# A quarter of each low part moved from VectorE to GpSimd in a float32 decoder trunk

## The chip, the cores and the metric

The kernel runs on one core of one Trainium2 chip. The metric is the device time of one execution in microseconds (us), the median over runs; lower is better.

## The reference

The reference is a decoder trunk in float32: 256 tokens of width 1024 pass through four layers. Cut to what matters:

```python
for i in range(4):
    x = x + 0.5 * swiglu(rms_norm(x, g[i, 0]), w_gate[i, 0], w_up[i, 0], w_down[i, 0])
    h = rms_norm(x, g[i, 1])
    q, k, v = split(h @ w_qkv[i], 3)
    mix = attention_i(q, k, v)           # stick-breaking, differential, forgetting, stick-breaking
    x = x + mix @ w_o[i]
    x = x + 0.5 * swiglu(rms_norm(x, g[i, 2]), w_gate[i, 1], w_up[i, 1], w_down[i, 1])
return rms_norm(x, final_g)
```

`swiglu(x)` is `(silu(x @ w_gate) * (x @ w_up)) @ w_down` with a hidden width of 2816. The weights are float32 and each is used once per execution.

## The kernel before

**Chunks.** All weights lie in DRAM as one stream of 328 chunks, each 128 partitions x 2048 float32 columns (1 MB). A feed-forward phase uses 33 chunks (for each of 11 units of the hidden width a `top` and a `bottom` chunk with gate and up columns, and a `down` chunk), an attention phase 16 (`v`, `q`, `k`, `o`). There are 12 phases: feed-forward, attention, feed-forward in each of the four layers. The chunk that opens a phase is called c0 here, the ones behind it c0+1, c0+2 and so on; the chunks are used in the order of the stream (`FFN_ORDER`, `ATT_ORDER`).

**Split in high and low parts.** A float32 product is made of three products in the rounded format `fp32r`: high x high, high x low, low x high. Each chunk c goes through four stations:

- SyncE issues its DMA into `raw[c % 3]` (`load`, L281), once the low part of chunk c-3 has been taken, since that frees the buffer. The first 12 loads are written out, the rest run in a hardware loop (L299 to L302).
- ScalarE rounds it into `w_hi[c % 6]` (`hi`, L338), after `slot_free` has seen TensorE finish with chunk c-6. It counts `hi_ready`.
- VectorE takes `w_lo = raw - w_hi` over all 2048 columns (`lo`, L548), after `hi_ready`. It counts `lo_ready`.
- TensorE waits for `lo_ready` and multiplies. `product` (L902 to L904) issues the three matmuls.

Chunk 0 is done in two halves (`first_hi`, `first_lo`, L344 to L347 and L555 to L559).

**What sets the order.** Every engine runs one list of instructions that is written out by hand; `split_to(c)` and `split_next(k)` put the `hi` and `lo` of coming chunks at fixed places between an engine's other work. VectorE's other work is: the elementwise product of the hidden activations (`scratch`, L612), the low part of the activations (`m_lo`, L591 in feed-forward, L702 and L720 in attention), the residual update (`x`, L828), the gained and turned input (`wide`, L834) and its low part (`xg`, L840), and in attention the scaling of q and k (`q_t`, `k_t`, L682), the rotation (L690 to L692), masks and row sums.

**GpSimd** has one task: the power -0.5 of the mean square, two elements for each partition (`r_col`, L318 for the 12 phases, L321 for the two at the end). It waits for `mean_ready`, which VectorE counts in `norm_mean` (L570). In a phase, VectorE's order is: low part of c0+2, `norm_mean`, low parts of c0+3 and c0+4 (in attention `norm_diag`, L576, which waits for `r_col`, stands between `norm_mean` and c0+3). The low parts of c0 and c0+1 are taken near the end of the phase before.

**Waits.** An instruction carries one wait itself; a further wait on the same engine is an instruction of its own (EVENT_SEMAPHORE in the trace).

Of the kernel before, what the change touches and what calls it, by code (L numbers as in the profile page):

```python
# [8 lines left out]
F32 = mybir.dt.float32  # L9
F32R = mybir.dt.float32r  # L10
ALU = mybir.AluOpType
# [13 lines left out]
FFN_CHUNKS = 3 * UNITS  # L25
ATT_CHUNKS = 4 * PAIRS
# [4 lines left out]
HALF_D = D // 2  # L31
FIRST_KS = DT // 2
PEELED = 4
RAW = 3
RING = 6
SCALE = HD ** -0.5
# [63 lines left out]
def trunk(nc, stream, x_in, gains, consts, lam_in, subln_in, wf_in, bf_in, final_in, out):  # L100
    with ExitStack() as ctx:
# [3 lines left out]
        def sem(name):  # L105
            return ctx.enter_context(nc.semaphore(name))
# [43 lines left out]
        ones_loaded, const_loaded, gain_loaded = sem("ones_loaded"), sem("const_loaded"), sem("gain_loaded")  # L150
        x_loaded = sem("x_loaded0"), sem("x_loaded1")
        hi_ready = sem("hi_ready")
        lo_ready = sem("lo_ready")
        top_used = sem("top_used")
        acc_ready = sem("acc_ready")
        x_updated = sem("x_updated")
# [121 lines left out]
        @block.sync  # L278
        def _(sp):
            def load(c, chunk):  # L280
                sp.dma_start(raw[:, c % RAW, :], stream[chunk]).then_inc(raw_loaded[c % RAW], 16)  # L281

            sp.dma_start(cst[:, 0:C_LATER], consts[:, 0:C_LATER]).then_inc(ones_loaded, 16)
            sp.dma_start(gain[:], gains).then_inc(gain_loaded, 16)
            for half in range(2):
                cols = slice(half * HALF_D, (half + 1) * HALF_D)
                sp.dma_start(x[:, :, cols], x_in[:, :, cols]).then_inc(x_loaded[half], 16)
                part = slice(half * HALF, (half + 1) * HALF)
                sp.dma_start(raw[:, 0, part], stream[0, :, part]).then_inc(raw_loaded[0] if half else raw_half_loaded, 16)
            for c in range(1, RAW):  # L290
                load(c, c)
            for c in range(RAW, PEELED * RAW):
                sp.wait_ge(lo_ready, c - RAW + 1)
                load(c, c)
            for tile, source in ((cst[:, C_LATER:], consts[:, C_LATER:]), (lam_q[:], lam_in), (subln[:], subln_in),
                                 (wf[:], wf_in), (bf[:], bf_in), (final_gain[:], final_in)):
                sp.dma_start(tile, source).then_inc(const_loaded, 16)
            rounds = CHUNKS // RAW - PEELED
            with sp.Fori(0, rounds) as turn:  # L299
                for k in range(RAW):  # L300
                    sp.wait_ge(lo_ready, turn * RAW + ((PEELED - 1) * RAW + k + 1))
                    load(RAW + k, turn * RAW + (PEELED * RAW + k))  # L302
            for c in range((rounds + PEELED) * RAW, CHUNKS):
                sp.wait_ge(lo_ready, c - RAW + 1)
                load(c, c)
            for i, bank in enumerate(banks_of(NORMS - 1)):
                cols = slice(bank // TB * HALF_D, (bank // TB + 1) * HALF_D)
                sp.wait_ge(y_ready, i + 1)
                sp.dma_start(out[:, bank % TB, cols], x_part(bank)).then_inc(stored, 16)
            sp.wait_ge(stored, 16 * BANKS)  # L310

        @block.gpsimd
        def _(pool):
            nc.gpsimd.memset(half_neg[:], -0.5).then_inc(const_ready, 1)
            pool.wait_ge(const_ready, 1)
            for n in range(NORMS - 1):
                pool.wait_ge(mean_ready, n + 1)
                nc.gpsimd.tensor_tensor(r_col[:], mean[:], half_neg[:], ALU.pow).then_inc(r_col_ready, 1)  # L318
            for tb in range(TB):
                pool.wait_ge(mean_ready, NORMS + tb)  # L320
                nc.gpsimd.tensor_tensor(r_col[:, tb:tb + 1], mean[:, tb:tb + 1], half_neg[:, tb:tb + 1],  # L321
                                        ALU.pow).then_inc(r_col_ready, 1)
# [212 lines left out]
        def _(dve):  # L535
# [9 lines left out]
            def lo(c, turn=0):  # L545

                dve.wait_ge(hi_ready, c + 1 + turn * RING)
                nc.vector.tensor_tensor(w_lo[:, c % RING, :], raw[:, c % RAW, :], w_hi[:, c % RING, :].bitcast(F32),  # L548
                                        ALU.subtract).then_inc(lo_ready, 1)

            def first_lo(half):
# [347 lines left out]
        def _(pe):  # L899
# [52 lines left out]
            def ffn(layer, n, c0, _, f):  # L952
# [25 lines left out]
                def first_step(u):  # L978

                    turn_part(n, 2)  # L980
                    pe.wait_ge(lo_ready, c0 + 1)
                    pe.wait_ge(xg_ready, BANKS * n + 1)
                    gate_up(u, 0, c0, top)
                    turn_part(n, 3)
                    pe.wait_ge(xg_ready, BANKS * n + 2)
                    gate_up(u, 1, c0, top).then_inc(top_used, 1)

                def step(s, c, turn):
                    u = f * UNITS + s
                    if s == 0:  # L990
                        first_step(u) if n else very_first_step(u)
                    else:
                        pe.wait_ge(lo_ready, c + 1 + turn * RING)
                        gate_up(u, 0, c, top)
                        gate_up(u, 1, c, top).then_inc(top_used, 1)
                        hidden(u - 1, turn)
                    pe.wait_ge(lo_ready, c + 2 + turn * RING)
                    for tb in range(TB):
                        if s == 0:
                            pe.wait_ge(xg_ready, BANKS * n + 3 + tb)  # L1000
                        gate_up(u, tb, c + 1, bottom).then_inc(gu_psum, 1)
                    if s == UNITS - 1:
                        unit_down(s - 1, c + 2, turn, (0, 1))
                        hidden(u, turn)
                        unit_down(s - 1, c + 2, turn, (2, 3)).then_inc(down_used, 1)
                    elif s:
                        unit_down(s - 1, c + 2, turn).then_inc(down_used, 1)
# [9 lines left out]
                def unit_down(s, c, turn, banks=(0, 1, 2, 3)):  # L1017
                    u = f * UNITS + s
                    if banks[0] == 0:
                        pe.wait_ge(lo_ready, c + 1 + turn * RING)  # L1020
                        pe.wait_ge(h_split, u + 1 + turn * 2)
                    return contract_pair(c, u % 2 * 2, s == 0, banks)

                def last_down():
                    u, c = f * UNITS + UNITS - 1, c0 + FFN_CHUNKS - 1
                    pe.wait_ge(lo_ready, c + 1)
                    pe.wait_ge(h_split, u + 1)
                    contract_last(c, u % 2 * 2, n + 1)

# [5 lines left out]
            def attention(layer, n, c0, _, kind):  # L1035
# [5 lines left out]
                def values(js):  # L1041

                    half = js[0] // 2
                    for part in range(2):
                        c = c0 + ATT_ORDER.index(("v", 2 * half + part))
                        pe.wait_ge(lo_ready, c + 1)
                        for j in js:
                            tokens = slice(j % TB * P, (j % TB + 1) * P)
                            if half == 0:
                                pe.wait_ge(xg_ready, BANKS * n + TB * part + j + 1)  # L1050
                            for k in range(part * FIRST_KS, (part + 1) * FIRST_KS):
                                ins = product(work[:, V_BANK[j], :], xg_hi[:, k, tokens], xg_lo[:, k, tokens],
                                              wide_chunk(w_hi, c)[:, k % FIRST_KS, :],
                                              wide_chunk(w_lo, c)[:, k % FIRST_KS, :], start=k == 0, stop=k == DT - 1)
                            if part:
                                ins.then_inc(v_psum, 1)
                            elif j == 0:
                                turn_part(n, 3)
# [15 lines left out]
                def head_projection(c, bank, h):  # L1074

                    pe.wait_ge(lo_ready, c + 1)
                    ins = project(work[:, bank, h * T:(h + 1) * T], c, h * P)
                    if h:
                        ins.then_inc(qk_psum, 1)
# [74 lines left out]
                def output(j, banks=(0, 1, 2, 3)):  # L1154
                    c, b = c0 + ATT_ORDER.index(("o", j)), first + j
                    if banks[0] == 0:
                        pe.wait_ge(lo_ready, c + 1)
                        pe.wait_ge(mix_ready, b + 1)
                    if j == PAIRS - 1:
                        contract_last(c, 2 * (b % 2), n + 1)  # L1160
                        return
                    ins = contract_pair(c, 2 * (b % 2), j == 0, banks)
                    if banks[-1] == 3:
                        ins.then_inc(out_used, 1)
# [125 lines left out]
```

## Time and profile before

| | us |
|---|---|
| median of 3 runs | 1994.91 (1994.75 to 1997.24) |
| the profiled execution's own time | 1994.82 |
| its span in the profile | 1993.0 |
| TensorE busy (matmuls) | 1963.7, 99% of the span |
| VectorE busy | 1089.1, 55% |
| ScalarE busy | 918.9, 46% |
| GpSimd busy | 25.5, 1% |
| mean granted TensorE clock | 0.994 of full speed |

The span is what the profiler saw from the first to the last instruction; the execution's own time is 1.8 us longer. Times in rows count from the start of the span. PE is TensorE (matmuls), PEld its weight loads, DVE is VectorE, ACT ScalarE, POOL GpSimd, SP SyncE.

### The profile page before, as it was taken

Reading aid. Unit: us, or ns where it says so; the run is one execution under the profiler, and the core shown is the slowest. Engines: PE = TensorE matmul, PEld = TensorE weight load, DVE = VectorE, ACT = ScalarE, POOL = GpSimd, SP = SyncE. Lnnn points to the kernel's source line nnn. Section 1 sums busy time; section 2 is a strip of 40 time slices with the busy share of each in tenths; the row PEclk is TensorE's granted clock in tenths of the full one; section 3 lists DMA queues with packets and bytes.
Section 4 is the critical chain, followed back from the end, with each engine's and each line's share of the span. In section 5 each row is a group of like instructions: output and inputs, shape, how many; then the busy total and the mean of one; then the engine's idle time right before and its main releaser. Section 6 shows DMA issues by size and latency. Waiting matters only on the chain.

```text
span 1993.0 us, 24383 instructions
## 1 busy us (share of the span) xinstructions
PE 1963.7 (99%) x9684; PEld 1651.2 (83%) x9684; DVE 1089.1 (55%) x999; ACT 918.9 (46%) x942; POOL 25.5 (1%) x19
## 2 busy tenths in 40 slices
PE   7999999999999999999999999999999999999998
PEld 5888898888888888788888889988888888988886
DVE  5544566554644567644465554764446455646444
ACT  5444565444544445544444443454444444555442
POOL 0000000000000000000000000000000000000000
PEclk9999999999999999999999998999999999999999
DMA  6554444454455452454545542545554544535551
GB/s 248 212 186 189 165 151 170 183 185 185 184 190 189 148 190 106 151 188 188 189 182 185 184 166 106 181 162 186 188 190 183 183 185 165 190 127 190 188 186 69
DMA packets 49711, 348.58 MB, mean 175 GB/s; under 512 B 6128, under 2 KB 6256, under 8 KB 7792
## 3 DMA queue, kind: packets, MB, share of 16 engines
q1 hardware_dynamic: 49648, 347.67, 47.3%
q8 instruction: 48, 0.79, 0.2%
q14 instruction: 15, 0.12, 0.0%
HBM read 346.60 MB, written 1.05 MB: 174 GB/s over the span
## 4 chain that ended last, share of the span: by engine, by line
PE 96%; DVE 2%; ACT 1%; issue 0%; DMA 0%; SPq 0%; DVEq 0%; POOLq 0%; POOL 0%; ACTq 0%
PE work L902 20%; PE work L904 20%; PE work L903 20%; PE acc L902 9%; PE acc L904 9%; PE acc L903 9%; PE work L1013 2%; PE acc L945 1%; DVE w_lo L548 1%; PE work L1142 1%; PE work L1129 0%; PE work L1069 0%; PE work L1120 0%; PE work L1084 0%; PE work L1143 0%
## 5 line engine op out<-in xcount | busy, mean ns | idle before, releaser
L548 DVE TENSOR_TENSOR w_lo<-raw,w_hi 128x2048 fp32r<-128x2048 f32 x327 | 741.6, 2289 | 224.2 <-ACT w_hi L338 224.2
L338 ACT ACTIVATE w_hi<-raw 128x2048 fp32r<-128x2048 f32 x327 | 613.8, 1906 | 19.7 <-DMA raw<-stream_dram 19.5
L902 PE MATMUL work<-w_hi,xg 128*128 128x512 f32 x1536 | 609.4, 397 | 7.5 <-DVE w_lo L559 3.8
L904 PE MATMUL work<-w_hi,xg 128*128 128x512 f32 x1536 | 600.5, 391 | 0.0
L903 PE MATMUL work<-w_lo,xg 128*128 128x512 f32 x1536 | 599.7, 390 | 0.0
L902 PEld LDWEIGHTS work<-w_hi,xg 128*128 128x128 f32 x1536 | 289.4, 188 | 65.9 <-DVE w_lo L555 4.1
L904 PEld LDWEIGHTS work<-w_hi,xg 128*128 128x128 f32 x1536 | 289.2, 188 | 62.0
L903 PEld LDWEIGHTS work<-w_lo,xg 128*128 128x128 f32 x1536 | 289.5, 188 | 57.4
L902 PE MATMUL acc<-w_hi,m_hi 128*128 128x512 f32 x832 | 330.0, 397 | 4.4 <-DVE m_lo L720 4.4
L904 PE MATMUL acc<-w_hi,m_lo 128*128 128x512 f32 x832 | 325.3, 391 | 0.0
L903 PE MATMUL acc<-w_lo,m_hi 128*128 128x512 f32 x832 | 324.9, 390 | 0.0
L360 ACT ACTIVATE m_hi<-work 128x512 fp32r<-128x512 f32 x88 | 52.7, 598 | 552.0 <-PE work L1013 552.0
L591 DVE TENSOR_TENSOR m_lo<-work,m_hi 128x512 fp32r<-128x512 f32 x88 | 60.8, 691 | 381.7 <-ACT m_hi L360 381.7
L902 PEld LDWEIGHTS acc<-w_hi,m_hi 128*128 128x128 f32 x832 | 156.9, 189 | 36.3 <-issue 5.2
L380 ACT ACTIVATE scratch<-work,r_col 128x256 f32<-128x256 f32 x176 | 83.5, 475 | 222.3 <-PE work L904 214.5
L904 PEld LDWEIGHTS acc<-w_hi,m_lo 128*128 128x128 f32 x832 | 156.7, 188 | 33.2
L903 PEld LDWEIGHTS acc<-w_lo,m_hi 128*128 128x128 f32 x832 | 157.0, 189 | 31.3
L902 PE MATMUL work<-xg,w_hi 128*128 128x256 f32 x512 | 149.5, 292 | 1.1 <-DVE m_lo L702 1.0
L904 PE MATMUL work<-xg,w_lo 128*128 128x256 f32 x512 | 145.6, 284 | 0.0
L903 PE MATMUL work<-xg,w_hi 128*128 128x256 f32 x512 | 145.6, 284 | 0.0
L612 DVE SCALAR_TENSOR_TENSOR scratch<-work,r_col,scratch 128x256 f32<-128x256 f32 x176 | 84.0, 481 | 72.9 <-ACT scratch L380 72.9
L902 PEld LDWEIGHTS work<-xg,w_hi 128*128 128x128 f32 x512 | 99.0, 193 | 3.0 <-DVE m_lo L702 1.7
(132 smaller groups left out, 1009.3 us busy)
## 6 DMA issues: line engine op xcount, KB each, us to landing
raw<-stream_dram SPq DMA_DIRECT2D x327, 1024.0 KB, 4.8
x<-x_dram SPq DMA_DIRECT2D x2, 512.0 KB, 5.1
raw<-stream_dram SPq DMA_DIRECT2D x2, 512.0 KB, 6.3
out_dram<-x SPq DMA_DIRECT2D x4, 256.0 KB, 2.6
cst<-consts_dram SPq DMA_DIRECT2D x1, 848.0 KB, 6.7
final_gain<-final_gain_dram SPq DMA_DIRECT2D x1, 512.0 KB, 6.5
cst<-consts_dram SPq DMA_DIRECT2D x1, 128.0 KB, 2.1
gain<-gains_dram SPq DMA_DIRECT2D x1, 52.0 KB, 2.2
```

The source lines that it names most:

```text
L338: nc.scalar.activation(w_hi[:, c % RING, :], raw[:, c % RAW, :], ACT.Copy).then_inc(hi_ready, 1)
L360: nc.scalar.activation(m_hi[:, u % 2 * 2:u % 2 * 2 + 2, :], halves(unit_bank(u, 0)), ACT.Copy).then_inc(h_hi_ready, 1)
L380: nc.scalar.activation(silu_sb[tb], unit_bank(u, tb)[:, 0:COLS], ACT.Silu, scale=r_col[:, tb:tb + 1]).then_inc(silu_ready, 1)
L548: nc.vector.tensor_tensor(w_lo[:, c % RING, :], raw[:, c % RAW, :], w_hi[:, c % RING, :].bitcast(F32), ALU.subtract).then_inc(lo_ready, 1)
L591: nc.vector.tensor_tensor(m_lo[:, u % 2 * 2:u % 2 * 2 + 2, :], halves(unit_bank(u, 0)), m_hi[:, u % 2 * 2:u % 2 * 2 + 2, :].bitcast(F32), ...
L612: nc.vector.scalar_tensor_tensor(out=h_sb[u % 2][tb], in0=unit_bank(u, tb)[:, COLS:2 * COLS], scalar=r_col[:, tb:tb + 1], in1=silu_sb[tb], ...
L902: nc.tensor.matmul(dst, a_hi, b_hi, start=start, stop=False, skip_group_check=skip)
L903: nc.tensor.matmul(dst, a_hi, b_lo, start=False, stop=False, skip_group_check=skip)
L904: return nc.tensor.matmul(dst, a_lo, b_hi, start=False, stop=stop, skip_group_check=skip)
L945: ins = nc.tensor.transpose(turned(bank)[:, d, :], x_part(bank)[:, d * P:(d + 1) * P], ident)
L1013: ins = nc.tensor.transpose(unit_bank(u, 0)[:, t * T + tb * P:t * T + (tb + 1) * P], h_sb[u % 2][tb][:, t * P:(t + 1) * P], ident)
L1142: nc.tensor.matmul(bank, v[:, 0, cols], w[:, 0:T], start=True, stop=True)
```

## The change

GpSimd takes columns 1536 to 2047 of the low part of every chunk but chunk 0 (`lo_rest`), and VectorE's `lo` keeps columns 0 to 1535. A new semaphore, `lo_rest_ready`, counts GpSimd's part. Since chunk 0 has none, its count is c once chunk c is done. Wherever TensorE waits for `lo_ready`, it now also waits for `lo_rest_ready`, and so does SyncE before it loads into a raw buffer; SyncE's loop of loads is written out. GpSimd's list becomes: for each phase, `lo_rest` of c0 and c0+1, then the wait for `mean_ready` and `r_col`, then `lo_rest` of c0+2 to the end of the phase. GpSimd's list is written out without a loop too.

```diff
+OWN = 1536
...
-        lo_ready = sem("lo_ready")
+        lo_ready, lo_rest_ready = sem("lo_ready"), sem("lo_rest_ready")
...
             for c in range(RAW, PEELED * RAW):
                 sp.wait_ge(lo_ready, c - RAW + 1)
+                if c > RAW:
+                    sp.wait_ge(lo_rest_ready, c - RAW)
                 load(c, c)
...
-            rounds = CHUNKS // RAW - PEELED
-            with sp.Fori(0, rounds) as turn:
-                for k in range(RAW):
-                    sp.wait_ge(lo_ready, turn * RAW + ((PEELED - 1) * RAW + k + 1))
-                    load(RAW + k, turn * RAW + (PEELED * RAW + k))
-            for c in range((rounds + PEELED) * RAW, CHUNKS):
+            for c in range(PEELED * RAW, CHUNKS):
                 sp.wait_ge(lo_ready, c - RAW + 1)
+                if c > RAW:
+                    sp.wait_ge(lo_rest_ready, c - RAW)
                 load(c, c)
...
-            for n in range(NORMS - 1):
-                pool.wait_ge(mean_ready, n + 1)
-                nc.gpsimd.tensor_tensor(r_col[:], mean[:], half_neg[:], ALU.pow).then_inc(r_col_ready, 1)
+            def lo_rest(c):
+
+                pool.wait_ge(hi_ready, c + 1)
+                nc.gpsimd.tensor_tensor(w_lo[:, c % RING, OWN:], raw[:, c % RAW, OWN:], w_hi[:, c % RING, OWN:].bitcast(F32),
+                                        ALU.subtract).then_inc(lo_rest_ready, 1)
+
+            for phase in phases():
+                n, c0 = phase[1:3]
+                count = ATT_CHUNKS if phase[3] else FFN_CHUNKS
+                for c in range(c0, c0 + count):
+                    if c:
+                        lo_rest(c)
+                    if c == c0 + 1:
+                        pool.wait_ge(mean_ready, n + 1)
+                        nc.gpsimd.tensor_tensor(r_col[:], mean[:], half_neg[:], ALU.pow).then_inc(r_col_ready, 1)
...
                 dve.wait_ge(hi_ready, c + 1 + turn * RING)
-                nc.vector.tensor_tensor(w_lo[:, c % RING, :], raw[:, c % RAW, :], w_hi[:, c % RING, :].bitcast(F32),
+                cols = slice(0, OWN)
+                nc.vector.tensor_tensor(w_lo[:, c % RING, cols], raw[:, c % RAW, cols], w_hi[:, c % RING, cols].bitcast(F32),
                                         ALU.subtract).then_inc(lo_ready, 1)
...
                         pe.wait_ge(lo_ready, c + 1 + turn * RING)
+                        pe.wait_ge(lo_rest_ready, c + turn * RING)
                         gate_up(u, 0, c, top)
```

The last pair of lines stands for all places on TensorE: each wait for `lo_ready` but chunk 0's gets a second one behind it.

## Rows read from the trace of the kernel before

**Rows 1.** The page: busy time by engine; shares of the chain that ended last

```profile
PE 1963.7 (99%) x9684; PEld 1651.2 (83%) x9684; DVE 1089.1 (55%) x999; ACT 918.9 (46%) x942; POOL 25.5 (1%) x19
...
PE 96%; DVE 2%; ACT 1%; issue 0%; DMA 0%; SPq 0%; DVEq 0%; POOLq 0%; POOL 0%; ACTq 0%
```

**Rows 2.** Busy time by stretch: length, PE, PEld, DVE, ACT, POOL, clock, DMA

```profile
20.00:1982.00 1962.00, 1952.86 (x9643) 1642.88 (x9644) 1076.97 (x981) 909.52 (x927) 24.07 (x12) 0.99 0.47 175
```

**Rows 3.** The costliest groups, VectorE's and ScalarE's; mean ns of one behind the comma

```profile
L548 DVE TENSOR_TENSOR w_lo<-raw,w_hi 128x2048 fp32r<-128x2048 f32 x327 | 741.6, 2289 | 224.2 <-ACT w_hi L338 224.2
L338 ACT ACTIVATE w_hi<-raw 128x2048 fp32r<-128x2048 f32 x327 | 613.8, 1906 | 19.7 <-DMA raw<-stream_dram 19.5
```

**Rows 4.** The chain in order of time (start, us): a step of every third chunk

```profile
36.16 0.44 PE work L1013 x4
52.97 0.44 PE work L1013 x4
```

**Rows 5.** Waits of the weight loads: us in total, times, longest us

```profile
PEld work L902 <- DVE m_lo L702: 1.7, 2, 1.4
...
PEld work L1084 <- DVE q_t L682: 0.4, 1, 0.4
PEld work L1084 <- DVE k_t L682: 0.4, 1, 0.4
...
PEld work L1116 <- DVE k_t L682: 0.3, 1, 0.3
```

**Rows 6.** The chain in order of time, in attention phases: low parts on it

```profile
705.85 2.20 DVE w_lo L548
...
1257.50 2.20 DVE w_lo L548
...
1736.50 2.20 DVE w_lo L548
```

**Rows 7.** Groups by shape: a VectorE subtraction of 512 columns

```profile
L591 DVE TENSOR_TENSOR m_lo<-work,m_hi 128x512 fp32r<-128x512 f32 x88 | 60.8, 691 | 381.7 <-ACT m_hi L360 381.7
```

**Rows 8.** Timeline of GpSimd (start us, us)

```profile
324.78 2.67 POOL L318 TENSOR_TENSOR r_col<-mean,half_neg 128x2 f32<-128x2 f32 x1 [110.32 <-DVE mean L570]
...
698.34 0.69 POOL L318 TENSOR_TENSOR r_col<-mean,half_neg 128x2 f32<-128x2 f32 x1 [184.10 <-DVE mean L570]
...
1984.35 0.55 POOL L321 TENSOR_TENSOR r_col<-mean,half_neg 128x1 f32<-128x1 f32 x1 [174.05 <-DVE mean L879]
```

**Rows 9.** Timeline of VectorE at the start of phase 2 (feed-forward)

```profile
322.35 2.29 DVE L548 TENSOR_TENSOR w_lo<-raw,w_hi 128x2048 fp32r<-128x2048 f32 x1
324.55 0.15 DVE L570 SCALAR_TENSOR_TENSOR mean<-sums 128x2 f32<-128x2 f32 x1
324.62 4.49 DVE L548 TENSOR_TENSOR w_lo<-raw,w_hi 128x2048 fp32r<-128x2048 f32 x2
...
335.07 0.69 DVE L591 TENSOR_TENSOR m_lo<-work,m_hi 128x512 fp32r<-128x512 f32 x1 [1.33 <-ACT m_hi L360]
```

**Rows 10.** Timeline of TensorE there: first weight load of c0+2; first `m_hi` matmul

```profile
328.14 0.19 PEld L902 LDWEIGHTS work<-w_hi,xg 128*128 128x128 f32 x1
...
339.71 0.39 PE L902 MATMUL acc<-w_hi,m_hi 128*128 128x512 f32 x1
```

**Rows 11.** Timeline of ScalarE there: high part of c0+5, and `m_hi`

```profile
329.49 1.92 ACT L338 ACTIVATE w_hi<-raw 128x2048 fp32r<-128x2048 f32 x1 [0.46 <-DMA raw<-stream_dram]
334.44 0.60 ACT L360 ACTIVATE m_hi<-work 128x512 fp32r<-128x512 f32 x1 [3.03 <-PE work L1013]
```

**Rows 12.** Timeline of VectorE in phase 1, chunk c0+5 of the attention

```profile
228.81 2.29 DVE L548 TENSOR_TENSOR w_lo<-raw,w_hi 128x2048 fp32r<-128x2048 f32 x1 [5.26 <-ACT w_hi L338]
```

**Rows 13.** Timeline of the weight loads there: the first of chunk c0+5

```profile
231.34 0.19 PEld L902 LDWEIGHTS work<-w_hi,xg 128*128 128x128 f32 x1
```

**Rows 14.** DMA issues of the chunks: KB each, median us from issue to landing

```profile
raw<-stream_dram SPq DMA_DIRECT2D x327, 1024.0 KB, 4.8
```

**Rows 15.** TensorE's line L1021: waits that are instructions (min/median/max ns)

```profile
L1021 PEldq EVENT_SEMAPHORE  x16: 51/51/51, 38.0 to 1969.9; - x16
```

More of the change, by code:

```diff
@@ L981, in first_step @@
                     pe.wait_ge(lo_ready, c0 + 1)
+                    pe.wait_ge(lo_rest_ready, c0)
                     pe.wait_ge(xg_ready, BANKS * n + 1)
@@ L997, in step @@
                     pe.wait_ge(lo_ready, c + 2 + turn * RING)
+                    pe.wait_ge(lo_rest_ready, c + 1 + turn * RING)
                     for tb in range(TB):
@@ L1020, in unit_down @@
                         pe.wait_ge(lo_ready, c + 1 + turn * RING)
+                        pe.wait_ge(lo_rest_ready, c + turn * RING)
                         pe.wait_ge(h_split, u + 1 + turn * 2)
@@ L1026, in last_down @@
                     pe.wait_ge(lo_ready, c + 1)
+                    pe.wait_ge(lo_rest_ready, c)
                     pe.wait_ge(h_split, u + 1)
@@ L1046, in values @@
                         pe.wait_ge(lo_ready, c + 1)
+                        pe.wait_ge(lo_rest_ready, c)
                         for j in js:
@@ L1076, in head_projection @@
                     pe.wait_ge(lo_ready, c + 1)
+                    pe.wait_ge(lo_rest_ready, c)
                     ins = project(work[:, bank, h * T:(h + 1) * T], c, h * P)
@@ L1157, in output @@
                         pe.wait_ge(lo_ready, c + 1)
+                        pe.wait_ge(lo_rest_ready, c)
                         pe.wait_ge(mix_ready, b + 1)
```

## The prediction

> **What bounds the kernel now.** I read the page first. TensorE is busy in 99% of the span and carries 96% of the chain that ended last [rows 1]. By stretches, it is idle for 1962.00 - 1952.86 = 9.1 us between 20 and 1982 us [rows 2]; the rest of its idle time lies in the first 20 us and in the last 11, which the change leaves alone but for chunks 1 and 2. So the most that any edit of VectorE can win in the middle is about 9 us, 0.46%. A chunk takes TensorE (52.97 - 36.16) / 3 = 5.60 us [rows 4], while VectorE needs 2.29 us for its low part and ScalarE 1.91 for its high part [rows 3]. Low parts are made well ahead of use, and their mean cost is hidden; what counts are single places where TensorE waits behind one.
>
> The waits of the weight loads name these places [rows 5]: before the rotation of q and of k in the differential layer (0.4 us each), before q times k in the last layer (0.3) and before the output product of the forgetting layer (1.4). In each of the four, the chain in order of time shows one or two whole low parts just ahead of the late VectorE result, six in all [rows 6]. The longest waits of TensorE in the middle, behind the normalisation in the differential layer, have no low part in front of them.
>
> **VectorE's part.** From 512 to 2048 columns a VectorE subtraction grows from 691 to 2289 ns [rows 7, 3], 1.04 ns a column. 1536 columns then take 2.29 - 0.53 = 1.76 us: 0.53 us less for each chunk, 174 us of VectorE's busy time over 327 chunks. Of this only what shortens a wait of TensorE reaches the end: the two waits of 0.4 and the one of 0.3 are covered whole by one or two times 0.53, of the 1.4 only 0.53 goes. Gain: 0.4 + 0.4 + 0.3 + 0.5 = **1.6 us**. Behind them nothing else is late: the ScalarE and TensorE steps that follow start earlier by as much.
>
> **What one GpSimd subtraction costs.** No row has it. The nearest row of this engine is its two-input operation of one element, 0.55 us [rows 8], which is the floor. The far end is the same engine's longest, 2.67 us [rows 8]. Between them I take the fixed 0.55 and VectorE's slope for 512 columns, **1.1 us**, since a subtraction lies nearer to VectorE's work than a power does. The Trainium skill (GPSIMD Engine Reference, section 3.1) measures 4497 ns for 2048 float32 columns against VectorE's 2293; a quarter would be 1.12 us, and the sum below would move by 0.2 us. No row here shows that rate.
>
> **Whether both engines work at once.** The same power of two elements takes GpSimd 0.69 us at 698.34 and 2.67 at 324.78 [rows 8]. In the second case VectorE's low part of c0+3 starts at 324.62 and is over at about 326.9 [rows 9], and the power ends 0.54 us after that, as if it had stood still until then. So a GpSimd operation waits while VectorE subtracts one SBUF tensor from another. No row shows the opposite, a VectorE subtraction behind a GpSimd one. I take it that it waits too, up to 1.1 us. The Trainium skill (SBUF — State Buffer, section on who interferes with whom) speaks against the change here: a VectorE instruction with two SBUF inputs and a GpSimd one that reads SBUF hold a shared port pair in turns, each for its whole duration. By that rule a chunk's low part is whole after 1.76 + 1.1 = 2.9 us, later than the 2.29 of before; the trace agrees for one of the two directions.
>
> In the steady part this costs nothing. A pair of turns takes 2.9 of 5.60 us, and the buffers free 0.6 us later for loads that take 4.8 us each [rows 14] with three in flight: (4.8 + 1.9 + 2.9) / 3 = 3.2 us per chunk against 5.60. If that cover were gone, it would be 0.6 us for each of 327 chunks. The VectorE steps that TensorE waits for, `m_lo`, `h` and x, read one tensor from PSUM and one from SBUF and should not compete; `xg` reads two from SBUF, but GpSimd has nothing to do then, as c0+1 is done and c0+2 comes behind the mean.
>
> **The start of a phase** is where the order of GpSimd's list tells. `lo_rest` of c0+2 stands behind `r_col`, which stands behind `norm_mean`, which VectorE reaches only after its own c0+2. In phase 2, with each low part 0.53 us shorter, VectorE's c0+2 runs from 322.35 to 324.11, c0+3 to 325.85 and c0+4 to 327.5 [rows 9]. The power is held until c0+3 is over and ends at 325.85 + 0.54 = 326.4. Then GpSimd's part of c0+2 is held behind VectorE's c0+4, and ends at 327.4 + 1.1 = 328.5. TensorE loads the first weights of c0+2 at 328.14 [rows 10]; before, the low part had been ready since 322.35 + 2.29 = 324.64. Loss: 0.35 us, in each of the seven feed-forward phases behind the first: **2.5 us**. In attention phases VectorE stands still for `r_col`, the power is quick (the 0.69 of rows 8), and there is 2 us of room. At the start of the kernel chunks 1 and 2 have 1.1 and 0 us of room by the same working: **0.15 us**.
>
> The load of c0+5 now waits for this late part: it starts at 328.5 in place of 324.6, lands 4.8 us later [rows 14], and ScalarE's high part of c0+5 ends at 335.2, where it ended at 331.4. `m_hi` stands behind it and started at 334.44 [rows 11], so it slips by 0.8 us, and `m_lo` with it from 335.8 to 336.6 [rows 9]. TensorE reads these at 339.71 [rows 10]: 3.1 us of cover, no loss.
>
> **Chunk c0+5 of the first attention** is the one chunk that arrives in time only just. VectorE takes it from 228.81 to 231.10 [rows 12], and TensorE loads its weights at 231.34 [rows 13]. In turns it is whole at 230.57 + 1.1 - 0.15 = 231.5, so **0.2 us** are lost.
>
> **The waits.** TensorE passes 33 new waits in each feed-forward and 26 in each attention phase, 368. Such a wait is 51 ns of the sequencer [rows 15], 19 us in all, which is hidden: `m_lo` ended at 335.76 and was read at 339.71 [rows 9, 10], and in the steady part matmuls follow each other over such waits, so the sequencer passes them while the array has work queued. Without this cover it would be 19 us. They are placed ahead of the late waits (`xg`, `m_lo`), not behind. **SyncE's list** without a loop costs nothing: it issues one load in 5.60 us, and its second wait stands ahead of it. GpSimd's pair at the end is unchanged.
>
> **Sum.** -1.6 + 2.5 + 0.15 + 0.2 = +1.2 us on the profiled execution's 1994.8 (its span of 1993.0 and 1.8 around it), which stands 0.1 under the median of the three runs: **1996.0 us**.
>
> **The rivals.**
> - *No taking of turns.* If the two subtractions overlap, VectorE's gain of 1.6 us is kept and the late parts come 1 us earlier, just in time: 1994.8 - 1.6 = 1993.2. For: only one direction of the holding is in the trace. Against: a power of two elements was held for 2 us. Chance 0.15, and still inside 0.2%.
> - *Slower: GpSimd's turn at the start of the phases.* If the subtraction takes T in place of 1.1 us, nine places (seven starts, chunk 2, the chunk of rows 12) lose T - 1.1 more each. It decides, that is passes 0.2% or 4 us, from T = 1.4. With T = 2.3, GpSimd as slow on its quarter as VectorE was on the whole, it is 9 x 1.2 = 10.8 more: 2006.8. At T = 2.67 it is 2010. For: seven starts with the same pattern, and next to no room in any. Against: the floor of 0.55. Chance 0.18. Beyond 5.6 us GpSimd would become the bound, at 327 us for each microsecond above; chance 0.02.
> - *The change does not do what it says.* Each VectorE low part that follows a GpSimd part waits for it, so that VectorE is busy for as long as before and the 1.6 us don't come, while the starts lose the same: 1994.8 + 2.9 = 1997.7. Chance 0.15, on the border of 0.1 to 0.2%.
> - *Faster by more than 0.2%* needs 4 us of the 9.1, more than all that stands behind low parts. Chance 0.05.
>
> **How the numbers follow.** About 0.2% is what a measurement of this kernel can tell from no change (its own three runs lie 0.12% apart). The forecast has 0.45; with the first and third rival, 0.75 lies within 0.2%, 0.05 is faster and 0.20 slower. The predicted time is the forecast's. The range goes down to the first rival with a little for the spread of runs, 1992.8, and up to T = 1.9, 9 x 0.8 = 7.2 above the forecast, 2003.
>
> **What would show it.** Right: `w_lo` on VectorE with a shortest duration of 1.76 us and some longer ones behind GpSimd; L318 near 2.1 us at seven starts; GpSimd's part of c0+2 ending at 328.5 and TensorE idle for a third of a microsecond before that chunk; the waits of rows 5 gone but for 0.9 of the 1.4. Wrong: GpSimd parts above 1.4 us, waits on `w_lo` in more places than nine, a pitch of matmuls longer at every added wait, or a granted clock that falls behind a new gap.

## The result and the profile after

The changed kernel took 2001.7 us in the median of ten runs, against 1995.31 us for the kernel before. The ratio is 1.0028, with a 95% interval of 1.0019 to 1.0036: slower by 0.28%, some 5.6 us. The profiled execution took 2001.54 us with a span of 1999.8, 6.7 us more (before rounding) than the 1993.0 of before. (The medians are over all ten runs of each, one far outlier in each among them; the ratio leaves such disturbed runs out.)

The page after, engines and chain, answers to [rows 1]:

```profile
PE 1968.3 (98%) x9684; PEld 1653.2 (83%) x9684; DVE 1009.2 (50%) x999; ACT 919.0 (46%) x942; POOL 853.5 (43%) x346
...
PE 93%; DVE 3%; POOL 2%; ACT 1%; issue 0%; DMA 0%; SPq 0%; DVEq 0%; POOLq 0%; ACTq 0%
```

VectorE lost only 80 of the 174 us of busy time that a quarter of the columns is worth, GpSimd is busy for 853 us, and it now has a share of the chain. The durations say why. The instructions of two lines of the kernel after, minimum, median and maximum in ns; they answer to the group of L548 in [rows 3] and to nothing before for GpSimd:

```profile
L319 POOL TENSOR_TENSOR w_lo<-raw,w_hi x327: 1259/2861/3221, 21.9 to 1969.1; 128x512 fp32r<-128x512 f32 x164
L561 DVE TENSOR_TENSOR w_lo<-raw,w_hi x327: 1736/1759/2892, 21.8 to 1968.0; 128x1536 fp32r<-128x1536 f32 x164
```

VectorE's low part takes 1.76 us when nothing holds it and up to 2.89 when something does (87 of the 327 are held by more than 0.1 us). GpSimd's quarter takes about 1.29 us alone and, in most cases, near 2.86 (256 of 327 take over 2.7): it stands until VectorE's low part of the same chunk is nearly over (1.76 - 0.15 + 1.29 = 2.90).

The start of phase 2, VectorE, GpSimd and the weight loads of the kernel after (start us, us); it answers to [rows 8 to 10], 1.4 us later in time:

```profile
323.60 1.75 DVE L561 TENSOR_TENSOR w_lo<-raw,w_hi 128x1536 fp32r<-128x1536 f32 x1
325.26 0.15 DVE L583 SCALAR_TENSOR_TENSOR mean<-sums 128x2 f32<-128x2 f32 x1
325.34 3.42 DVE L561 TENSOR_TENSOR w_lo<-raw,w_hi 128x1536 fp32r<-128x1536 f32 x2
```

```profile
325.50 2.14 POOL L330 TENSOR_TENSOR r_col<-mean,half_neg 128x2 f32<-128x2 f32 x1 [11.38 <-DVE mean L583]
...
327.60 2.30 POOL L319 TENSOR_TENSOR w_lo<-raw,w_hi 128x512 fp32r<-128x512 f32 x1
```

```profile
329.16 0.19 PEld L917 LDWEIGHTS work<-w_hi,xg 128*128 128x128 f32 x1
330.02 0.19 PEld L915 LDWEIGHTS work<-w_hi,xg 128*128 128x128 f32 x1 [0.67 <-issue]
```

GpSimd's part of c0+2 ends at 329.90, and the weight load that needs it starts at 330.02. Loads are 0.23 us apart in the stream, so it would have started at 329.39: 0.6 us late. The chain in order of time now runs through that place, from VectorE's c0+2 over `r_col` and GpSimd's part to TensorE:

```profile
323.68 1.67 DVE w_lo L561
325.35 0.08 DVE mean L583
325.43 0.07 issue
325.50 2.14 POOL r_col L330
327.64 2.28 POOL w_lo L319
329.91 0.14 issue
330.05 0.47 PE work L915
```

**Where the 6.7 us went.** Both profiles hold the same 9684 matmuls in the same order, so the start of each can be compared with itself. The distance between the two grows in few places:

| place (time after) | us |
|---|---|
| first 25 us | +1.4 |
| first chunk c0+2 of the seven later feed-forward phases (330 to 1817) | +3.9, 0.5 to 0.6 each |
| forget logits, 64 small matmuls of 8 columns for the forget gates (1208 to 1220) | +1.6 |
| forgetting layer, bias and output product (1238, 1266) | +0.7 |
| all other places, differential and stick-breaking layers (0.4 of it at 813 to 815) | -0.9 |

The first and the third row are in stretches where the granted clock is low. The busy time of the stretches 0 to 40 and 1200 to 1230 us, with the granted clock in the third number from the end, of the kernel before and then of the kernel after:

```profile
0.00:40.00 40.00, 26.85 (x108) 21.71 (x109) 21.57 (x20) 22.67 (x27) 2.91 (x6) 0.96 0.70 257
1200.00:1230.00 30.00, 30.00 (x194) 28.84 (x193) 11.16 (x25) 11.57 (x11) 0.00 (x0) 0.83 0.35 132
```

```profile
0.00:40.00 40.00, 26.88 (x102) 21.64 (x103) 18.44 (x19) 21.31 (x26) 12.35 (x11) 0.91 0.65 233
1200.00:1230.00 30.00, 30.00 (x181) 28.90 (x180) 9.89 (x11) 10.78 (x12) 6.75 (x6) 0.77 0.30 106
```

A mean of 0.83 over 30 us is 10.2 us at the lower level (half of full speed), 0.77 is 13.7. At the start, the full level is first granted at 14.86 us before and at 16.20 after, and the low stretch behind it lasts 3.4 and 6.8 us. A third low stretch, of 6.8 us in both, ends at 813.6 before and at 814.9 after; TensorE reaches this place 2.2 us later, so fewer of its matmuls fall into the stretch, and that gives back the 0.4 us at 813 to 815. So 1.4 + 1.6 - 0.4 = 2.6 us of the difference are time at 1.2 GHz in place of 2.4.

### The profile page after: what moved, and what is told of

It is laid out like the page before. It is cut to its first block, busy times and chain, and to the rows that moved or that the text cites. A ratio compares the mean times of both kernels' runs of the same rounds, so it can differ in the third digit from the quotient of the medians.

```text
span 1999.8 us, 24268 instructions
## 1 busy us (share of the span) xinstructions
PE 1968.3 (98%) x9684; PEld 1653.2 (83%) x9684; DVE 1009.2 (50%) x999; ACT 919.0 (46%) x942; POOL 853.5 (43%) x346
## 4 chain that ended last, share of the span: by engine, by line
PE 93%; DVE 3%; POOL 2%; ACT 1%; issue 0%; DMA 0%; SPq 0%; DVEq 0%; POOLq 0%; ACTq 0%
PE work L915 20%; PE work L917 19%; PE work L916 19%; PE acc L915 9%; PE acc L917 9%; PE acc L916 9%; PE work L1029 2%; DVE w_lo L561 1%; PE acc L958 1%; POOL w_lo L319 1%; POOL r_col L330 1%; PE work L1162 1%; PE work L1088 1%; PE work L1149 1%; PE work L1163 0%
## 5 line engine op out<-in xcount | busy, mean ns | idle before, releaser
L319 POOL TENSOR_TENSOR w_lo<-raw,w_hi 128x512 fp32r<-128x512 f32 x327 | 834.0, 2564 | 966.1 <-ACT w_hi L350 966.1
L561 DVE TENSOR_TENSOR w_lo<-raw,w_hi 128x1536 fp32r<-128x1536 f32 x327 | 650.2, 1991 | 264.9 <-ACT w_hi L350 261.9
```

The source lines that it names most:

```text
L319: nc.gpsimd.tensor_tensor(w_lo[:, c % RING, OWN:], raw[:, c % RAW, OWN:], w_hi[:, c % RING, OWN:].bitcast(F32), ALU.subtract).then_inc(lo_ ...
L561: nc.vector.tensor_tensor(w_lo[:, c % RING, cols], raw[:, c % RAW, cols], w_hi[:, c % RING, cols].bitcast(F32), ALU.subtract).then_inc(lo_ ...
```

## The experiments

Theories to begin with. **A**: the loss is the order at the seven starts; GpSimd's part of c0+2 stands behind `r_col`, and both stand behind VectorE's low parts. **B**: each chunk pays a little, by the added waits, by GpSimd's work as such or by the taking of turns (a subtraction on one engine standing still until that of the other is over). Open besides: why the gain of 1.6 us did not come, and whether the low-clock stretches belong to the change.

### GpSimd's part of c0+2 ahead of r_col

```diff
-                    if c == c0 + 1:
+                    if c == c0 + 2:
                         pool.wait_ge(mean_ready, n + 1)
```

> GpSimd's list is changed in one place: its part of c0+2 comes ahead of the wait for the mean and of r_col, not behind. Theory (the loss lies at the starts of the seven feed-forward phases behind the first, where this part is late): the seven idle stretches of TensorE of 0.44 us before chunk c0+2 are gone, and the time falls by 7 x 0.55 = 3.9 us against the changed kernel, to about 1998. Rival (every chunk pays a little, through the added waits or the taking of turns): the time stays at the changed kernel's 2001 to 2002.

Measured: 1995.45 us, ratio to the kernel before 0.9998 (0.9989 to 1.0007), span 1993.0. GpSimd and the weight loads at the start of phase 2:

```profile
309.58 4.12 POOL L319 TENSOR_TENSOR w_lo<-raw,w_hi 128x512 fp32r<-128x512 f32 x2 [15.01 <-ACT w_hi L350]
323.85 2.14 POOL L330 TENSOR_TENSOR r_col<-mean,half_neg 128x2 f32<-128x2 f32 x1 [10.15 <-DVE mean L583]
```

```profile
327.51 0.19 PEld L917 LDWEIGHTS work<-w_hi,xg 128*128 128x128 f32 x1
327.73 0.19 PEld L915 LDWEIGHTS work<-w_hi,xg 128*128 128x128 f32 x1
```

GpSimd's parts of c0+1 and c0+2 now start 14 us before `r_col`, and TensorE goes from one chunk to the next without a gap; the same holds for all seven starts. Moving one instruction undid the whole loss. It won more than the expected 3.9 us: the profiled execution also has the low-clock stretches of the kernel before (0.96 in the first 40 us, 0.83 at the forget logits), and none of the eleven runs has a mean clock below 0.993, where six of the changed kernel's nine (the outlier aside) have 0.992. Theory A stands, and B cannot hold a loss that one move of an instruction takes away: the waits, the work and the turns are all still there.

### Half of the columns, and an eighth

```diff
-OWN = 1536
+OWN = 1024
```

> GpSimd takes 1024 columns in place of 512, VectorE 1024. Theory (order at the start): GpSimd's one part grows from 1.29 to about 2.0 us, but VectorE's three low parts ahead of it shrink by 0.53 us each, so GpSimd's part of c0+2 ends earlier than TensorE needs it and the seven idle stretches are gone; the first attention's chunk c0+5 is late by 0.6 us, and attention chains behind held VectorE low parts lose some 1 us: about 1999. Rival (GpSimd's work as such costs): twice the columns, twice the loss, about 2008.

Measured: 2005.21 us, ratio 1.0046 (1.0032 to 1.0059). The seven gaps are gone, as A says, yet the time is 6 us above its expectation and nearer to the rival's 2008. The waits of the weight loads tell where:

```profile
PEld work L1162 <- DVE q_t L705: 5.8, 3, 2.7
...
PEld work L1124 <- DVE scratch L676: 2.3, 1, 2.3
```

VectorE and then GpSimd in the differential layer, at the first of the three waits for the rotated q:

```profile
736.77 3.14 DVE L561 TENSOR_TENSOR w_lo<-raw,w_hi 128x1024 fp32r<-128x1024 f32 x1
740.01 2.70 DVE L703 TENSOR_TENSOR q_t<-q_t,cst 32x512 f32<-32x512 f32 x1
742.64 0.67 DVE L704 TENSOR_TENSOR wide<-work,cst 32x512 f32<-32x512 f32 x1
743.34 2.41 DVE L705 TENSOR_TENSOR q_t<-q_t,wide 32x512 f32<-32x512 f32 x1
```

```profile
736.41 5.76 POOL L319 TENSOR_TENSOR w_lo<-raw,w_hi 128x1024 fp32r<-128x1024 f32 x2 [7.58 <-ACT w_hi L350]
742.86 2.35 POOL L319 TENSOR_TENSOR w_lo<-raw,w_hi 128x1024 fp32r<-128x1024 f32 x1 [0.69 <-ACT w_hi L350]
```

The rotation steps L703 and L705 read two SBUF tensors and took 0.68 us each before; here they take 2.70 and 2.41 while GpSimd subtracts. L704, which reads one of its inputs from PSUM, keeps its 0.67. The expectation had put such held VectorE work at 1 us in all. So the excess does not come chunk by chunk, as B has it: what a GpSimd subtraction costs is set by which VectorE instruction stands behind it.

```diff
-OWN = 1536
+OWN = 1792
```

> GpSimd takes 256 columns, VectorE 1792. Theory (order at the start): GpSimd's one part shrinks from 1.29 to about 0.9 us, but VectorE's three low parts ahead of it grow by 0.27 us each, so the seven idle stretches grow by about 0.4 us each: 3 us above the changed kernel, about 2004.5. Rival (GpSimd's work as such costs): half the columns, about half the loss, 1998 to 1999.

Measured: 2001.8 us, ratio 1.0022 (1.0013 to 1.0031), where the changed kernel had 1.0028 (1.0019 to 1.0036): the two can't be told apart, and neither the 2004.5 nor the 1998 to 1999 came. The trace has to decide. The weight loads at the start of phase 2:

```profile
328.51 0.19 PEld L917 LDWEIGHTS work<-w_hi,xg 128*128 128x128 f32 x1
329.61 0.19 PEld L915 LDWEIGHTS work<-w_hi,xg 128*128 128x128 f32 x1 [0.91 <-DVE w_lo L561]
```

The gap there is 0.9 us, against 0.67 with 512 columns and none with 1024. By the starts of the matmuls each of the seven places loses about 0.8 us in place of 0.55. The direction is A's and against B's; the size was overstated (0.2 us more for each place, not 0.4), as I had put GpSimd's 256 columns at 0.9 us and they take 0.73. This is the plainest evidence for the mechanism: the loss falls as GpSimd's share rises, because VectorE's three low parts ahead in the line become shorter.

### The quarter left out

```diff
-                    if c:
+                    if 1 <= c < RING:
                         lo_rest(c)
...
-                        pe.wait_ge(lo_rest_ready, c + turn * RING)
+                        pe.wait_ge(lo_rest_ready, min(c, RING - 1))
```

(and so at all waits for `lo_rest_ready`).

> The last quarter of the low part is computed for chunks 1 to 5 only; for all later chunks it is left out (the ring keeps the old values), so GpSimd does nothing but r_col. VectorE keeps 1536 columns, the waits stay. Theory (the gain of 1.6 us was there, and GpSimd's turns took it back): 1.6 us below the kernel before, about 1993.5, with the waits before the rotations and before q times k of the last layer gone. Rival (a shorter low part on VectorE wins nothing, or the added waits cost): the kernel before's time or above.

Measured: 1994.93 us, ratio 0.9992 (0.9983 to 1.0001), span 1992.3, 0.7 below before. VectorE's low parts are all at 1735 to 1760 ns, and of the waits of [rows 5] the two before the rotations and the one before q times k are gone, the one before the output product has gone from 1.4 to 0.8 us. Yet by the starts of the matmuls these four places win only 0.8 us together: 0.3 before the rotation of q and 0.5 before the output product. The 0.3 before the rotation of k is taken back within 1 us by a longer wait for ScalarE, and the 0.4 before q times k within 1.3 us by a new wait for `m_lo`. The wait for ScalarE before and here, and the waits for `m_lo` here (three, where [rows 5] has two):

```profile
PEld work L1150 <- ACT scratch L438: 3.3, 4, 1.1
```

```profile
PEld work L1170 <- ACT scratch L450: 3.6, 4, 1.1
...
PEld work L915 <- DVE m_lo L715: 1.4, 3, 0.8
```

Three places that the prediction does not name win 0.15 us each. At the end of three attention phases TensorE waited for the residual update, which stood behind a whole low part on VectorE (309.80 to 312.09 in the first). This wait of the kernel before is gone in all kernels in which the low part is shorter there:

```profile
PEld acc L945 <- DVE x L828: 1.1, 3, 0.4
```

So the attention phases win 0.8 + 0.45, or 1.3 us. Of this, 0.6 us are given back at chunk 2, the c0+2 of the first phase, where the order of the seven starts loses an eighth time. GpSimd and the weight load of chunk 2 in this kernel (timelines of 20 to 36 and of 31 to 32.4 us):

```profile
27.34 2.30 POOL L330 TENSOR_TENSOR r_col<-mean,half_neg 128x2 f32<-128x2 f32 x1 [3.26 <-DVE mean L583]
29.61 5.39 POOL L319 TENSOR_TENSOR w_lo<-raw,w_hi 128x512 fp32r<-128x512 f32 x3
```

```profile
31.01 0.19 PEld L915 LDWEIGHTS work<-w_hi,xg 128*128 128x128 f32 x1 [0.74 <-issue]
```

The gain is real, but too small to be told from the runs alone. The added waits and the unrolled loads are in this kernel too: they cost nothing that can be seen.

### GpSimd only writes

```diff
-                nc.gpsimd.tensor_tensor(w_lo[:, c % RING, OWN:], raw[:, c % RAW, OWN:], w_hi[:, c % RING, OWN:].bitcast(F32),
-                                        ALU.subtract).then_inc(lo_rest_ready, 1)
+                if c < RING:
+                    ...
+                else:
+                    pool.wait_ge(lo_rest_ready, c - 1)
+                    nc.gpsimd.memset(spare[:], 0.0).then_inc(lo_rest_ready, 1)
```

> The changed kernel, but from chunk 6 on GpSimd's instruction is a memset of 440 columns of a tile of its own (it reads nothing from SBUF); the last quarter of the low part is left out from there on. Theory (a GpSimd instruction and a VectorE subtraction of two SBUF tensors wait for each other because both read through one port): no VectorE low part is held, all at 1.76 us, no memset is held, and TensorE has no idle stretch before chunk c0+2, since the memset is short and free; time 1993.5 to 1995.5, as with the quarter left out. Rival (any GpSimd activity holds VectorE): low parts of 2.2 us and more stay in the trace, and waits of the attention phases with them.

Measured: 1994.72 us, ratio 0.9998 (0.9989 to 1.0007), span 1992.5. The durations of the two instructions:

```profile
L325 POOL MEMSET spare<- x322: 460/467/473, 41.3 to 1960.7; 128x440 f32 x161
L566 DVE TENSOR_TENSOR w_lo<-raw,w_hi x327: 1735/1759/2821, 21.2 to 1960.7; 128x1536 fp32r<-128x1536 f32 x164
```

322 memsets stay within 460 to 473 ns although 293 of them run beside one of VectorE's subtractions, and from chunk 6 on no low part is held (the 2821 is one of the first five chunks, where GpSimd still subtracts). So GpSimd's activity as such holds nothing; what held VectorE, and was held, were GpSimd instructions that read two SBUF tensors. One that reads a single tensor was not tried. The Trainium skill (SBUF — State Buffer, section on who interferes with whom) has this as an exclusive lock on a shared port pair, which a VectorE instruction with two SBUF inputs takes against a GpSimd one that reads, not against one that only writes. These runs agree, in both directions.

### Attention phases on VectorE alone

```diff
-                cols = slice(0, OWN)
+                cols = slice(0, OWN if SHARED[c] else CHUNK)
...
-                    if c:
+                    if SHARED[c]:
                         lo_rest(c)
```

(`SHARED` is true for the chunks of feed-forward phases; the counts of the waits are adjusted, and c0+2 stands ahead of `r_col`.)

> As the first experiment (GpSimd's part of c0+2 ahead of r_col), and in the four attention phases VectorE takes whole low parts; GpSimd takes its quarter in feed-forward phases alone. Theory (outside the starts, the change acts only in attention phases, where it wins 0.3 to 0.5 us in the differential layer and loses 0.9 us in the forgetting layer, whose VectorE work is held): against the kernel before, TensorE's starts stay within 0.2 us at every place, the waits of rows 5 are back at 0.4, 0.4, 0.3 and 1.4 us, time within 0.5 us of the kernel before. Rival (GpSimd costs something in the steady part as well): above it by more than 1 us.

Measured: 1995.12 us, ratio 0.9999 (0.999 to 1.0008), span 1993.9. The waits are back at what they were in [rows 5]:

```profile
PEld work L923 <- DVE m_lo L723: 1.7, 2, 1.4
PEld work L1112 <- DVE q_t L703: 0.4, 1, 0.4
PEld work L1112 <- DVE k_t L703: 0.4, 1, 0.4
...
PEld work L1144 <- DVE k_t L703: 0.3, 1, 0.3
```

Behind the first 25 us no matmul is displaced against the kernel before by more than 0.15 us at one place; the three displacements of that size are the gains at the ends of attention phases, where the low part ahead of the residual update is already one of the next feed-forward phase. So in feed-forward phases 263 GpSimd quarters, most of them held for 1.6 us, cost nothing, and the other effects of the change lie in the attention phases and at their ends. The first 25 us cost 1.2 us here as well, with a granted clock of 0.91, and as the start of the kernel is the same as in the first experiment, which has 0.96, this varies from execution to execution.

### The kernel before, made late

```diff
-                    for t in range(2):
+                    for t in range(2) if u != 4 * UNITS else [0, 1] * 7:
```

> The kernel before, with four transposes in the first feed-forward phase of layer 2 issued seven times in place of once: 24 transposes more, 2.6 us of TensorE, and everything behind is late by that. Theory (the changed kernel lost 1.5 us at the forget logits only because it reached them 2.9 us late, and the granted clock's low stretch there then fell longer, 13.7 us in place of 10.2): 2.6 + 1.5 = 4.1 us above the kernel before in the profile, with a low stretch of 13.7 us. Rival (the 1.5 us came from GpSimd's work around the forget logits): 2.6 us above, low stretch 10.2 us.

Measured: 1996.58 us, ratio 1.0007 (0.9998 to 1.0017), span 1995.8: 2.8 above before, of which the start is 1.4 and the delay 2.6, and the rest comes back at the forget logits, where the low stretch was 6.8 us, shorter than before. The number of 13.7 missed, but not the claim that timing moves the stretch: this kernel does nothing on GpSimd but `r_col`. With four and with six issues in place of seven:

> The kernel before, with the four transposes issued four times in place of once, 1.3 us of TensorE. So far the length of the low-clock stretch at the forget logits went with how long after the first logit matmul the clock fell: 2.6 and 2.8 us after, 13.7 us low; 3.9 to 4.4, 10.2; 5.2, 6.8. Theory (timing alone sets the length, GpSimd's work has no part in it): this run falls into the same pattern; if the start of the kernel adds its 1.2 to 1.4 us again, the forget logits come 2.7 us late, as in the changed kernel, and the stretch is 13.7 us. Rival (the long stretch needs GpSimd's work): never 13.7 us in a kernel without it.

> The same with six issues, 2.2 us. Same theories: without the start's 1.2 to 1.4 us the logits come 2.2 us late and the clock falls some 3 us behind their start, so 13.7 us low; with them 3.5 us late, and 6.8 or 10.2 us.

Measured: 1998.05 us (ratio 1.0010, 1.0000 to 1.0019) with four, 1996.18 us (1.0007, 0.9997 to 1.0017) with six. The stretch 1200 to 1230 us of the two:

```profile
1200.00:1230.00 30.00, 30.00 (x183) 28.96 (x183) 9.05 (x11) 10.45 (x11) 0.69 (x1) 0.77 0.28 106
```

```profile
1200.00:1230.00 30.00, 30.00 (x201) 28.59 (x200) 11.39 (x24) 11.81 (x11) 0.69 (x1) 0.89 0.34 120
```

The kernel that is late by 1.3 us has the changed kernel's 0.77, without any low part on GpSimd, and costs 4.1 us of span for 1.3 us of added work: 1.2 at the start and 1.6 at the logits. The one late by 2.2 us has 0.89 and costs 0.5. The expectation for it, 13.7 us, missed too, as the clock fell 5.5 us behind the first logit matmul and not 3. One profile does not stand for its kernel here: the ten runs with six issues lie between 1995.03 us at a mean clock of 0.995 and 2000.38 at 0.992. Over all profiles the order holds: a fall 2.6 to 2.9 us behind the first logit matmul goes with 13.7 us of low clock (three profiles), 3.9 to 4.4 with 10.2 (six), 5.1 to 5.5 with 6.8 (two). The fall itself lies at 1209.52 us in the kernel before and at 1210.87 in the changed one. It is later by 1.35 us, as was the first grant of the full level at the start, while TensorE reaches the logits 2.9 us later. What decides when the clock falls in a given execution stays open.

## Why the prediction was right, and where it was not

The time was forecast as 1996.0 with a range of 1992.8 to 2003.0 and 0.75 for no difference beyond 0.2%. It came out at 0.28% above: in the range, but not in the likeliest case; being slower had 0.20. That the range held it is in part luck. Its upper end was set for a GpSimd subtraction of 1.9 us, and the subtraction takes 1.29; what carried the time above the forecast were starts of 3.9 us in place of 2.5, 2.6 us of low clock that the sum did not have, and a gain that came to nothing.

**The starts of the phases: right, and nearly to the size.** Forecast were seven starts with a loss of 0.35 us each; measured are seven with 0.5 to 0.6. GpSimd's part of c0+2 was to end at 328.5; it ends at 329.90, which is 328.5 on the clock of before, as everything there is 1.4 us later. L330 was to be near 2.1 us and has 2.137 in the median. Short was the step from that end to TensorE: I let the weight load start at once, and it came 0.12 us later, and TensorE would have been there 0.15 us sooner than I put it (329.39, where 328.14 and the 1.4 make 329.54). In the sum this term was 2.5 and measured 3.9. The 0.15 us for chunks 1 and 2 was the same pattern put too low: with the quarter left out and with GpSimd only writing, where the clock at the start is that of the kernel before and `r_col` stands ahead of chunk 2, chunk 2 loses 0.6 us. In the changed kernel's own profile `r_col` took 0.70 us there, held by nothing, and no loss is seen.

**The price of a GpSimd subtraction: right by luck.** I took a fixed 0.55 us and VectorE's slope, 1.1 us; the runs have 0.73, 1.29 and 2.35 us for 256, 512 and 1024 columns, that is 2.1 ns a column and 0.2 us fixed. Both parts were off and nearly cancelled. A quarter of the Trainium skill's 4497 ns (GPSIMD Engine Reference, section 3.1) is an estimate of 1.12 us, 0.17 below the measured 1.29.

**Turns in both directions: right**, and shown by the profile after (low parts of 2.7 to 2.9 us) and by the run in which GpSimd only writes.

**The gain of 1.6 us: the step that failed.** Two things were wrong with it. The first: "Behind them nothing else is late" does not hold. With the quarter left out and every low part at 1.76 us, the four places that I named win 0.8 us and not 1.6, since two of the waits are taken back by the next ones behind them; 0.45 us came from the three waits for the residual update, which I had not read. The 1.3 us that these make together are near the 1.6 by luck. The second: I counted each low part on the chain at 1.76 us, as if GpSimd held none. In the changed kernel the two rotation waits and the one before q times k shrank by only 0.3 us together, from 1.1 to 0.8, and the largest grew: before the output product of the forgetting layer VectorE's low part took 2.61 us, behind a GpSimd part that began 0.27 us earlier. In the kernel after, VectorE, GpSimd and the waits of the weight loads:

```profile
1262.32 2.61 DVE L561 TENSOR_TENSOR w_lo<-raw,w_hi 128x1536 fp32r<-128x1536 f32 x1
1264.85 0.68 DVE L715 TENSOR_TENSOR m_lo<-work,m_hi 128x512 fp32r<-128x512 f32 x1
```

```profile
1262.05 1.27 POOL L319 TENSOR_TENSOR w_lo<-raw,w_hi 128x512 fp32r<-128x512 f32 x1 [0.60 <-ACT w_hi L350]
```

```profile
PEld work L915 <- DVE m_lo L715: 2.0, 2, 1.7
...
PEld work L1104 <- DVE q_t L695: 0.3, 1, 0.3
PEld work L1124 <- DVE k_t L695: 0.3, 1, 0.3
PEld work L1104 <- DVE k_t L695: 0.2, 1, 0.2
```

At 1233 us the forget bias, also held, loses another 0.3. Against the 0.45 us won at the ends of three attention phases and 0.1 in the differential layer stand 0.7 lost in the forgetting layer, so nothing is left of the gain. The rule of turns was in my text, and I applied it to the time at which a chunk is whole but not to the VectorE instructions on the chain. A third rival said this in part (the gain does not come); it had 0.15 and a total of 1997.7.

**Left out: the clock.** Net 2.6 of the 6.7 us are time at the lower clock: 1.4 at the start and 1.6 at the forget logits, less 0.4 at 813 to 815. The list of signs named a clock that falls behind a new gap, and this is not that: the gaps are 0.7 us, and no low stretch follows one. The start's part comes without the change too: the kernels before made late by 2.6 and by 1.3 us have the same first 25 us as the kernel before, and lose 1.4 and 1.2 us there. The part at the logits goes with when they are reached and when the clock falls, and the kernel before has it as well when made late by 1.3 us. Of the changed kernel's nine runs (the outlier aside) six had a mean clock of 0.992, one 0.993 and two 0.994, these with 1999.10 and 2000.61 us; the kernel before, run beside the experiments, is never below 0.993. So part of the 0.28% is clock in the runs as well. How much, as a mean over runs, is not settled; in the profiles it is 2.6 us, the seven starts 3.9.

**Cover: right.** The high part of c0+5 slipped, ScalarE waiting 4.5 us for its load, and `m_hi` with it, and TensorE read `m_hi` without a gap. The first attention's chunk c0+5 was to lose 0.2 us; no loss is seen there. The waits and SyncE's list cost nothing.

**No version beats both.** With the quarter left out altogether the time is 0.08% below the kernel before, inside the noise. By its profile the shorter low parts are worth 1.3 us where GpSimd holds nothing, so no placement of GpSimd's part can be expected to win more than that here.

## What to carry to other kernels

Work that is moved to an idle engine enters a line of its own: ask what stands ahead of it in that engine's list and what that in turn waits for, and put the new piece ahead of the late wait; here one move of one instruction was the whole difference between a loss and none. When two engines hold each other's reads, count every instruction of either on the chain at its held duration, not only the piece that was moved. And when the bound engine is busy for 99% of the span, the ceiling of the edit is in the waits of that engine alone: 1.3 us, where VectorE's busy time promised 174. A wait that ends sooner is worth only what the next wait behind it leaves: of 1.6 us forecast at four waits, 0.8 came.

## What the runs showed that was not expected

A VectorE `tensor_scalar` from SBUF to SBUF is held as well: the sixteen of the forget bias took 3.22 us in all before and 4.63 in the kernel after, where a GpSimd part ran beside them. The loss at each of the seven starts falls when GpSimd gets more columns (about 0.8 us with 256, 0.5 to 0.6 with 512, none with 1024). And a delay of TensorE is not paid at its size: added work of 1.3 us cost 4.1 us of span in one profile and 2.2 us cost 0.5 in another, through the length of the low-clock stretch at the forget logits and in the first 25 us.
